# Moving half of the weight-split subtractions of the first dense stage from VectorE to GpSimd

## What is computed

```python
mod = (c @ p['w_ada'][l] + p['b_ada'][l])[:, None, :]          # 6 x 1024 columns of modulation
sh1, sc1, g1, sh2, sc2, g2 = jnp.split(mod, 6, axis=-1)
hm = rmsnorm(x, p['norm_mix'][l]) * (1.0 + sc1) + sh1
proj = h @ w_in                                                # rglru_mixer: 1024 x 2048 weights
y_br = jax.nn.gelu(proj[..., :D_RNN])
xr, new_buf = causal_conv(proj[..., D_RNN:], conv_buf, conv_w, conv_b)
```

## Time and profile before

| what | us |
|---|---|
| three runs | 2788.88, 2794.98, 2794.08 |
| median of the runs | 2794.08 |
| profiled execution, first to last instruction (span) | 2791.7 |
| median less span: what lies around the instructions, and the spread | 2.4 |
| first dense stage, from its first dense matmul to its last modulation matmuls | 53.57 to 155.87 |
| of that, one even and one odd round (starts at 93.08, 99.20, 104.68) | 6.12 and 5.48 |

### The profile page before, as it was taken

One profiled execution on the slowest core, in us unless ns is written; L12 is line 12 of the kernel. 1 busy time (PEld: TensorE's weight loads), 2 busy tenths in 40 slices (PEclk: granted clock), 3 DMA queues, 4 the chain that ended last, 5 costly groups with the idle time before them and its releaser, 6 DMA issues. The chain is left out here.

```text
span 2791.7 us, 50744 instructions
## 1 busy us (share of the span) xinstructions
PE 2530.5 (91%) x17672; PEld 2236.5 (80%) x17672; DVE 1823.1 (65%) x3955; ACT 1552.8 (56%) x3124; POOL 263.3 (9%) x240
## 2 busy tenths in 40 slices
PE   6978999999867999997989998899999976899997
PEld 3658988888756999997765534798899975899997
DVE  6844789866798555557244455349885479755555
ACT  5635655676696555556413542255556579555554
POOL 0000444100000000000001110014440000000000
PEclk8989999999988999999989999999999988999999
DMA  6743444577301455553206986344445510355452
GB/s 235 256 135 139 155 162 152 209 251 260 136 0 47 180 181 180 180 181 126 64 30 247 344 327 243 121 162 155 159 164 175 180 59 0 108 179 181 180 180 106
DMA packets 65102, 455.79 MB, mean 163 GB/s; under 512 B 8656, under 2 KB 8864, under 8 KB 10224
## 3 DMA queue, kind: packets, MB, share of 16 engines
q1 hardware_dynamic: 52128, 379.61, 38.5%
q0 software_dynamic: 11120, 73.29, 6.8%
q10 hardware_dynamic: 1760, 1.68, 0.2%
HBM read 415.27 MB, written 39.27 MB: 163 GB/s over the span
## 5 line engine op out<-in xcount | busy, mean ns | idle before, releaser
L824 ACT ACTIVATE w_parts<-ring 128x512 fp32r<-128x512 f32 x1376 | 851.4, 630 | 856.0 <-PE ps L423 767.0
L1199 DVE TENSOR_TENSOR w_parts<-ring,w_parts 128x512 fp32r<-128x512 f32 x1232 | 853.8, 704 | 606.1 <-ACT w_parts L824 597.3
L423 PE MATMUL ps<-h_hi,w_parts 128*128 128x264 f32 x5376 | 1022.7, 289 | 83.3 <-DVE w_parts L1199 58.0
L423 PEld LDWEIGHTS ps<-h_hi,w_parts 128*128 128x128 f32 x5376 | 854.9, 191 | 123.7 <-issue 68.7
L423 PE MATMUL ps<-h_lo,w_parts 128*128 128x264 f32 x2688 | 770.7, 287 | 0.0
L423 PE MATMUL ps<-g_parts,w_parts 128*128 128x264 f32 x6144 | 749.6, 284 | 7.5 <-DVE g_parts L1495 7.5
L423 PEld LDWEIGHTS ps<-g_parts,w_parts 128*128 128x128 f32 x6144 | 749.3, 189 | 7.8 <-issue 7.8
L423 PEld LDWEIGHTS ps<-h_lo,w_parts 128*128 128x128 f32 x2688 | 515.4, 192 | 2.0
L423 PE MATMUL ps<-SCR 128*128 128x128 f32 x1056 | 185.5, 331 | 92.4 <-DVE SCR L1466 85.2
L1126 POOL TENSOR_TENSOR w_parts<-ring,w_parts 128x512 fp32r<-128x512 f32 x144 | 210.9, 1466 | 479.6 <-ACT w_parts L824 479.2
L423 PEld LDWEIGHTS ps<-SCR 128*128 128x128 f32 x1056 | 158.9, 231 | 118.8 <-issue 87.9
(11 more groups left out here) (176 smaller groups left out, 1473.3 us busy)
## 6 DMA issues: line engine op xcount, KB each, us to landing
ring<-in_stream SPq DMA_DIRECT2D x362, 1024.0 KB, 4.8
BIG<-in_C POOLq DMA_DIRECT2D x32, 1024.0 KB, 8.5
out_C_s<-BIG POOLq DMA_DIRECT2D x32, 1024.0 KB, 5.9
out_C_p<-BIG POOLq DMA_DIRECT2D x16, 256.0 KB, 2.3
x<-in_x ACTq DMA_DIRECT2D x1, 1056.0 KB, 15.0
out_y<-BIG POOLq DMA_DIRECT2D x1, 1056.0 KB, 4.2
consts<-in_consts ACTq DMA_DIRECT2D x1, 256.0 KB, 10.4
BIG<-in_gates POOLq DMA_DIRECT2D x1, 192.0 KB, 2.7
```

Source lines behind the costliest of these rows:

```text
L423: return nc.tensor.matmul(out, lhsT, rhs, start=start, stop=stop, skip_group_check=shared)
L824: return nc.scalar.activation(to, of, f, **kw_)
L1199: tt(w_lo[:, j % HALVES, :], half_of(n, half), w_hi[:, j % HALVES, :].bitcast(F32), ALU.subtract).then_inc(lo_ready[half], 1)
```

## The change

GpSimd makes the odd `w_lo` of the 47 tiles behind the first (its queue gets them ahead of the wait on the recurrence); VectorE's loop makes the even ones only. Two waits keep the counts in order: GpSimd starts when VectorE has made the first tile's odd half, and VectorE goes into `peer(0)` only when the odd count of the stage is complete.

```diff
+            n0, j0 = FIRST["lru_in"], HALF["lru_in"]
+            pool.wait_ge(lo_ready[1], j0 // 2 + 1)
+            for t in range(1, 6 * NC):
+                j = j0 + 2 * t + 1
+                pool.wait_ge(hi_ready, j + 1)
+                nc.gpsimd.tensor_tensor(w_lo[:, j % HALVES, :], half_of(n0 + t, 1),
+                                        w_hi[:, j % HALVES, :].bitcast(F32), ALU.subtract)\
+                    .then_inc(lo_ready[1], 1)
+
             pool.wait_ge(hs_ready, NC)
...
             for t in range(6 * NC):
                 if t + 1 < 6 * NC:
-                    low(n0 + t + 1, j0 + 2 * t + 2)
+                    low(n0 + t + 1, j0 + 2 * t + 2, halves=1)
                 if t % 12 == 11:
                     copy_part(0, j0 + 2 * t)
...
             def peer(l):
+                if l == 0:
+                    dve.wait_ge(lo_ready[1], HALF["wq0"] // 2)
                 norm(2 * l + 1, f"norm_ffn{l}", l, 3, f"wq{l}")
```

## The result

The changed kernel takes 2801.17 us (median of 7 runs, 2797.82 to 2803.34) beside 2792.74 (7 runs) for the kernel before: ratio 1.0033, 95% interval 1.0023 to 1.0042, that is slower by 6.4 to 11.7 us. The forecast was 2807 in a range of 2796 to 2816: right in sign and range, 13 us forecast for the 8 to 9 that came.

The account below looks back on a forecast made before the run. The prediction saw TensorE as the overall bound, and a TensorE-ScalarE-VectorE loop pacing the first dense stage. Between walks summing to +8.6 and +17.7 us it took +13: span 2791.7 to 2804.7, plus 2.4 for runs, 2807; range 2796 to 2816.

Parts of the forecast that it names:

- The relief: First dense stage: taking 47 subtractions off VectorE gains nothing in even rounds; as rival, down to 2786 us, chance 0.03.
- The length of the subtraction: First dense stage: b1 takes 1.29 us on GpSimd, delaying c0 by 0.25 in odd rounds, hidden in even ones.
- The turns: VectorE's two-SBUF-input instructions and GpSimd's subtractions alternate on something shared: GpSimd holds it 1.15 us, VectorE's subtraction 0.55.
- Even round, 6.47: First dense stage: b1's hold on GpSimd delays VectorE's tap, then c0; 6.47 us, +0.35, hidden in three of eight rounds.
- Odd round, a toss-up between E+0.91 and E+0.87: E ends c1's matmuls; VectorE wants b0 at E+0.91, GpSimd b1 at E+0.87: +0.89 or +2.04 us a round.
- VectorE first: Odd rounds: VectorE's b0 precedes GpSimd's b1, c0 at E+3.41; 6.37 us, +0.89 a round, 8.6 us in sum.
- the other walk: Odd rounds: GpSimd's b1 precedes VectorE's b0, c0 at E+4.56; 7.52 us, +2.04 a round, 17.7 us in sum.
- A sign of being wrong: First dense stage: c0 waiting for GpSimd's b1 rather than for VectorE would show a chain, not turns; no size given.
- The end, +0.6: Last round of the stage: nothing hides the longer subtraction, +0.6 us with VectorE going first.
- No meeting that matters: Rival for the first dense stage: turns fall into idle time, +2.4 us, 2796.5 us; chance 0.13.
- Whole-length holds: Rival: both engines keep the shared thing to their ends, 1.29 and 0.69 us; +21 us, 2815 us; chance 0.10.
- The clock: Rival: more gaps bring TensorE's granted clock down in the stage, some 45 us at the worst; chance 0.04.

Follow-up runs that it names:

- e2: The changed kernel with one input of VectorE's subtractions and taps in the stage's loop read from PSUM instead of SBUF; 2798.05 us in one run.
- the control: The kernel before with one input of VectorE's subtractions and taps in the stage's loop read from PSUM instead of SBUF; 2791.17 us in one run.
- e3: The changed kernel with b1 of every round subtracted by VectorE again, GpSimd keeping c1 and a1; ratio 0.9999.
- e4: The changed kernel with GpSimd subtracting b1 alone, c1 and a1 back on VectorE; 2793.74 us in one run.
- e7: The changed kernel with ScalarE's eviction behind the next round's c0 and c1 copies and VectorE's taps one tile later; 2815.82 us in one run.
- e6: e3 with ScalarE's eviction moved behind its copies of the next round's c0 and c1, and VectorE's taps one tile later; ratio 1.0030.
- e5: The kernel before with ScalarE's eviction moved behind its copies of the next round's c0 and c1, and VectorE's taps one tile later; ratio 0.9984.

## Why the prediction was right, and what in it was off

- **The relief is worth nothing.** Right. It is less than nothing in one sense: VectorE's recorded busy time in the twelve rounds rose by 1.16 us with 36 instructions fewer. Without turns, in e2, an even round is 0.08 shorter than in the control, so little is there to win.
- **The length of the subtraction, +0.25 in odd rounds and 0 in even ones.** Right: e2 gives +0.22 and -0.08.
- **The turns, 1.15 and 0.55.** Right. The rows show them, and e2 shows what they cost. In the stage a hold of GpSimd's was 1.09 (89.01 less 87.92), and the tap let GpSimd in after 0.34 (a1 ended at 90.64, so began at 89.35), as estimated. b0 let b1 in after 0.54 (93.66 less 1.28 is 92.38, and b0 began at 91.84).
- **Even round, 6.47.** 6.46, and again nothing in the rounds with copies (7.26 before and after). The tap ended up behind b1's hold, as walked (99.33 less 98.25, 1.08).
- **Odd round, a toss-up between E+0.91 and E+0.87.** Here is the step that failed, the middle between two walks. With E at 91.17, VectorE issued b0 at 91.84, E+0.67; GpSimd got to b1 at 92.10, E+0.93. VectorE went first, and by the starts of b0 and b1 it did so in all odd rounds (6.25 us in the fourth round, then 6.15 or 6.16). My sum had counted the tap with 0.65 where 0.53 stands (the last one has no wait behind it) and holds of 1.15 for 1.09. So the walk "VectorE first" held throughout, with 6.15 instead of its 6.37: b0 is out of the way earlier, GpSimd's b1 begins at E+1.22 instead of 1.42, c0's own subtraction begins 1.13 behind that (92.85 + 1.36 - 0.69 = 93.52), and c0 starts when TensorE is done with b1, E+3.19. The middle between the two walks, 13, was a choice, and the other walk never came up in the changed kernel.
- **A sign of being wrong that came.** The prediction named c0 waiting for GpSimd's b1 as the sign of a chain instead of turns. In the odd round it is there: TensorE waits 0.49 for b1 and goes from it to c0 without a wait. But c0's subtraction ended at 94.21, 0.15 ahead, as in the even round, where TensorE did wait for it (100.67 and 100.82). So both paths end together, and b1 itself was late by a turn. e2, where that chain alone is left, prices it: 0.22 of the 0.67.
- **The end, +0.6.** It was +2.1. The last matmuls start 0.9 later, of which e2, without turns, has 0.62, as forecast. The other 1.2 came because the granted clock fell while they ran. In e2 they took 2.75 and in e3 and e4 1.95, so this part is a matter of when the fall comes, and the sum of the prediction had no term for it.
- **Luck in the sum.** The walk with VectorE first gave 8.6 and the stage 8.45, but not by the same terms. Odd rounds were to lose 6.2 and lost 4.1, the second round of the stage nothing (6.85 before and after); even ones were to lose 1.75 and lost 1.3 behind the first; the end had 2.1 instead of 0.6, and the first round's 0.92 isn't shown to be the change's.
- **The rivals.** "No meeting that matters" would have been 2.4; e2's 0.88 in twelve rounds is what it priced. "Whole-length holds" are out by the holds measured. The relief never won, in no order. The clock stayed at 1.00 in the twelve rounds; it cost 1.2 us at the end, and behind the third round it fell within the rounds in e7 alone, whose odd rounds were the longest.

In the difference 13 us were forecast and 8.4 came between the medians: the odd rounds, forecast at 10.3 by the middle (7 times the mean of 0.89 and 2.04), lost 4.1, which takes off more than that, and the end gave some back.

## What to carry to other kernels

Moving a two-input SBUF instruction from VectorE to GpSimd took 0.62 us off VectorE's queue here and put holds of about 1.1 us in its way; while VectorE still had two-input SBUF work queued, it finished no earlier, and the loss grew with what stood behind the meeting. Before offloading, ask whether the loaded engine sets the pace at all: a stage with VectorE 82% busy got 4 us shorter in twelve rounds by moving an eviction and a tap behind the next tile's work, with no engine relieved. And where a sum hangs on who comes first by 0.04 us, name the two outcomes and forecast one, since here the same order came in every odd round.

## What the runs showed that I had not expected

- An 8-column instruction pays the full price of a meeting: 1.25 us instead of 0.22, because GpSimd got in between it and the 256 columns ahead of it.
- The price of the same split depends on order far more than on amount: c1 and a1 on GpSimd cost 1.2 us in twelve rounds in one order (e3) and 9.7 in another (e6 against e5).
